# A recurrent mixer's decay factors grown in place by block products, its score grams cut to 32-column groups

## The reference

```python
b = jnp.cumsum(lc, axis=2)                       # lc: log forget
diff = b[:, :, :, None, :] - b[:, :, None, :, :]
decay = jnp.where(tri, jnp.exp(jnp.where(tri, diff, 0.0)), 0.0)
A = jnp.einsum('bhtd,bhsd,bhtsd->bhts', qc, kc, decay)
o = (jnp.einsum('bhts,bhsv->bhtv', A, vc)
     + jnp.einsum('bhtd,bhdv->bhtv', qc * jnp.exp(b), S))
S = (jnp.exp(b_last[:, :, 0, :])[..., None] * S
     + jnp.einsum('bhsd,bhsv->bhdv', kc * jnp.exp(b_last - b), vc))
```

## Time and profile before

| | |
|---|---|
| median of 3 runs | 1780.14 us |
| the profiled execution: its time, its span | 1781.3 us, 1779.7 us |
| PE, DVE, ACT, POOL busy | 1709.6, 940.2, 658.2, 307.3 us |
| mean granted PE clock | 0.989 |

### The profile page before, as it was taken

One profiled execution on the slowest core, in us unless ns is written; L12 is line 12 of the kernel. 1 busy time (PEld: TensorE's weight loads), 2 busy tenths in 40 slices (PEclk: granted clock), 3 DMA queues, 4 the chain that ended last, 5 costly groups with the idle time before them and its releaser, 6 DMA issues.

```text
span 1779.7 us, 33926 instructions
## 1 busy us (share of the span) xinstructions
PE 1709.6 (96%) x12754; PEld 1619.7 (91%) x12754; DVE 940.2 (53%) x1593; ACT 658.2 (37%) x1057; POOL 307.3 (17%) x362
## 2 busy tenths in 40 slices
PE   5999999989999999999999998888899999999997
PEld 5999999969999999999999997555589999999997
DVE  5788888875455555332443434444455555554221
ACT  4544444533433333222333444333333333333111
POOL 3222222212222222000000001111012222221000
PEclk8999999989999999999999999999999999999999
DMA  4222222212222222222233352555613222222331
GB/s 173 62 81 76 72 72 74 70 51 84 87 83 82 82 82 80 82 87 86 91 116 119 97 174 73 184 186 190 197 48 87 84 82 82 82 82 82 106 92 39
DMA packets 79236, 171.76 MB, mean 97 GB/s; under 512 B 6738, under 2 KB 40802, under 8 KB 79170
## 3 DMA queue, kind: packets, MB, share of 16 engines
q1 hardware_dynamic: 73218, 149.84, 27.4%
q0 software_dynamic: 5952, 21.02, 3.4%
HBM read 158.56 MB, written 12.27 MB: 96 GB/s over the span
## 4 chain that ended last, share of the span: by engine, by line
PE 89%; DMA 3%; DVE 2%; issue 2%; ACT 1%; SPq 1%; POOL 0%; DVEq 0%; ACTq 0%; POOLq 0%
PE acc L1353 75%; PE aux L1380 3%; DMA dec_Kd<-cache_k_in 3%; PE acc L1565 2%; PE acc L1583 1%; PE aux L1597 1%; SPq L351 1%; PE aux L1513 1%; PE aux L1441 1%; PE aux L1434 1%; PE aux L1388 1%; DVE xl L713 1%; PE acc L1573 1%; PE aux L1393 1%; PE aux L1419 0%
## 5 line engine op out<-in xcount | busy, mean ns | idle before, releaser
L1353 PE MATMUL acc<-xl,w_hi 128*128 128x288 f32 x2192 | 488.0, 304 | 21.6 <-DVE w_lo L707 16.6
L1353 PE MATMUL acc<-xh,w_hi 128*128 128x288 f32 x2192 | 472.0, 297 | 0.0
L1353 PE MATMUL acc<-xh,w_lo 128*128 128x288 f32 x2192 | 471.6, 297 | 0.0
L707 DVE TENSOR_TENSOR w_lo<-w_raw,w_hi 128x1024 fp32r<-128x1024 f32 (+1 forms) x217 | 283.6, 1307 | 337.6 <-ACT w_hi L382 334.2
L1353 PEld LDWEIGHTS acc<-xl,w_hi 128*128 128x128 f32 x2192 | 355.2, 190 | 35.1 <-DVE w_lo L707 17.3
L1353 PEld LDWEIGHTS acc<-xh,w_lo 128*128 128x128 f32 x2192 | 355.8, 190 | 0.0
L1353 PEld LDWEIGHTS acc<-xh,w_hi 128*128 128x128 f32 x2192 | 355.7, 190 | 0.0
L382 ACT ACTIVATE w_hi<-w_raw 128x1024 fp32r<-128x1024 f32 (+1 forms) x217 | 224.2, 1033 | 240.3 <-PE acc L1353 206.0
L1353 PE MATMUL acc<-ffn_glo,w_hi 128*128 128x288 f32 x704 | 151.0, 295 | 0.0
L1353 PE MATMUL acc<-ffn_gh,w_lo 128*128 128x288 f32 x704 | 149.8, 293 | 0.0
L1353 PE MATMUL acc<-ffn_gh,w_hi 128*128 128x288 f32 x704 | 148.9, 293 | 0.0
(11 more groups left out here) (250 smaller groups left out, 2449.6 us busy)
## 6 DMA issues: line engine op xcount, KB each, us to landing
w_raw<-w_fi_in SPq DMA_DIRECT2D x88, 512.0 KB, 3.6
w_raw<-w_mix_in SPq DMA_DIRECT2D x32, 512.0 KB, 3.6
w_raw<-w_fo_in SPq DMA_DIRECT2D x32, 512.0 KB, 3.5
dec_Kd<-cache_k_in SPq DMA_DIRECT2D x32, 512.0 KB, 6.9
dec_Vd<-cache_v_in SPq DMA_DIRECT2D x32, 512.0 KB, 5.9
w_raw<-w_kv_in SPq DMA_DIRECT2D x17, 512.0 KB, 3.7
w_raw<-w_o_in SPq DMA_DIRECT2D x16, 512.0 KB, 3.6
w_raw<-w_qg_in SPq DMA_DIRECT2D x16, 512.0 KB, 3.6
```

What stands on the lines that cost most here:

```text
L707: nc.vector.tensor_tensor(w_lo[:, pos.slot % SPL, 0:width], w_raw[:, pos.slot, 0:width], w_hi[:, pos.slot % SPL, 0:width].bitcast(F32), AL ...
L1353: mm = nc.tensor.matmul(acc[:, tp, hf, 0:HALF], W[:, sp_, 128 * j:128 * j + 128], X[:, kt, HALF * hf:HALF * hf + HALF], start=(first and j ...
```

## The change

The cumulated logs, their scan, differences and exponentials go. ACT makes f = exp(log f) once a head (`forget`, tile fd). On DVE the factors grow from level to level: `grow` multiplies, in place, k of each left block by the whole decay of the right block and qd (q times f at first) of each right block by the whole decay of the left one, and a third product makes the decays of blocks twice as long (tile dk). After seven levels qd is q exp(b) and k is k exp(b_last - b), so eb and kd go too. The levels now come in the order 1, 2, 4, ... 64, and gram g is k with qd as they stand after g-1 growths. Since a level below 32 has its pairs inside 32 tokens, grams 0 to 5 compute only the diagonal 32x32 blocks, each of the four in its own group of 32 columns of PE, into a narrow tile Ad (`take`, 160 or 128 columns); `diagonal_blocks` moves Ad into A later; grams 6 and 7 compute just the blocks beside it, which are copied without a mask. The samples ride along in grams 0 to 3. All grams and their evaluation use one PSUM bank. `grow` overwrites what gram g reads, so it stands behind `take` g, and gram g+1 waits for it (z_ok). The places in `quarters`, the state products and `new_state` move, and the state products now wait for og.

```diff
 
+        DK_AT = {1: 0, 2: 0, 4: 288, 8: 432, 16: 504, 32: 536, 64: 552, 128: 560}
+
+        def decay(par, m):
+            n = (T if m <= 8 else SEQ) // m
+            return fd[:, par, :] if m == 1 else dk[:, DK_AT[m]:DK_AT[m] + n]
...
+            def forget(t, par):
+
+                act.wait_ge(lf_ok, t + 1)
+                wait(act, z_ok, 8 * (t - 1))
+                nc.scalar.activation(fd[:, par, :], fl[:], ACT.Exp).then_inc(fd_ok, 1)
+                act.wait_ge(kd0_ok, t + 1)
+                wait(act, kT_ps, t - 1)
+                nc.scalar.activation(k_[:, par, :], kd0[:], ACT.Exp).then_inc(k_ok, 1)
...
-            def diff(hd, rp, j):
...
-            def zed(hd, rp, j):
...
+            def grow(hd, rp, j):
+
+                m = 1 << j
+                kv, qv = level(k_[:, rp], m), level(qd[:, rp], m)
+                n = kv.shape[1]
+                dm_ = decay(rp, m)[:, 0:2 * n].rearrange("p (n two) -> p n two", two=2)
+                dve.wait_ge(z_ok, 8 * hd + j + 1)
+                wait(dve, dk_ok, 7 * hd + j)
+                if j == 0:
+                    dve.wait_ge(fd_ok, hd + 1)
+                nc.vector.tensor_tensor(kv[:, :, 0, :], kv[:, :, 0, :], dm_[:, :, 1:2].to_broadcast([P, n, m]), ALU.mult)
+                nc.vector.tensor_tensor(qv[:, :, 1, :], qv[:, :, 1, :], dm_[:, :, 0:1].to_broadcast([P, n, m]), ALU.mult)\
+                    .then_inc(z_ok, 1)
+                if m == 4:
+                    wait(dve, s0_mul, hd)
+                if m == 64:
+                    wait(dve, s_step, 4 * hd)
+                nc.vector.tensor_tensor(decay(rp, 2 * m).rearrange("p (n one) -> p n one", one=1)[:, 0:n],
+                                        dm_[:, :, 0:1], dm_[:, :, 1:2], ALU.mult).then_inc(dk_ok, 1)
 
             def take(hd, g):
 
                 wait(dve, gram_used, 8 * hd + g)
-                dve.wait_ge(gram_ps, 8 * hd + g + 1)
+                dve.wait_ge(gram_ps, 8 * hd + max(g + 1, 2))
                 nc.vector.sem_inc(taking, 1)
-                mk = masks[:, g:g + 1, :]
-                if g in SAMPLE_GRAM:
-                    nc.vector.copy_predicated(As[:], masks[0:NS, SAMPLE_GRAM[g], 0:NS], aux[0:NS, 2, P - NS:P])
-                nc.vector.copy_predicated(A[:], mk.to_broadcast([P, NCH, P]),
-                                          aux[:, g % 2, :].rearrange("p (c s) -> p c s", c=NCH)).then_inc(gram_used, 1)
+                if g < 6:
+                    n = NCH + (g < 4)
+                    at = 160 if g == 1 else 0
+                    nc.vector.copy_predicated(Ad[:, 0:n, :], masks[:, g:g + 1, :].to_broadcast([P, n, 32]),
+                                              aux[:, 1, at:at + 32 * n].rearrange("p (c s) -> p c s", c=n)).then_inc(gram_used, 1)
+                elif g == 6:
+                    for x in (0, 2):
+                        r = slice(32 * x, 32 * x + 32)
+                        tc = nc.vector.tensor_copy(A[r, :, 32 * x + 32:32 * x + 64],
+                                                   aux[r, 1, 0:P].rearrange("p (c s) -> p c s", c=NCH))
+                    tc.then_inc(gram_used, 1)
+                else:
+                    nc.vector.tensor_copy(A[0:64, :, 64:128], aux[0:64, 1, 0:256].rearrange("p (c s) -> p c s", c=NCH))\
+                        .then_inc(gram_used, 1)
+
+            def diagonal_blocks(hd):
+
+                dve.wait_ge(gram_used, 8 * hd + 6)
+                wait(dve, o_ps, hd)
+                for x in range(4):
+                    r = slice(32 * x, 32 * x + 32)
+                    nc.vector.tensor_copy(A[r, :, r], Ad[r, 0:NCH, :])
+                for x in range(2):
+                    r = slice(32 * x, 32 * x + 32)
+                    tc = nc.vector.tensor_copy(As[r, r], Ad[r, NCH, :])
+                tc.then_inc(a_ok, 1)
 
...
-                    new_state(1)
                     dve.wait_ge(oh_ok, td + 1)
                     nc.vector.tensor_tensor(tile_of(ol, td), og[:], tile_of(oh, td).bitcast(F32), ALU.subtract)\
                         .then_inc(ol_ok, 1)
                 if rec:
-                    take(hd, 0)
+                    take(hd, 3)
+                    grow(hd, rp, 2)
+                if tail:
+                    new_state(0)
                 if front:
+                    wait(dve, fd_ok, t)
                     logsig(fr, fl, f_t, lf_ok, t)
-                    dve.wait_ge(lf_ok, t + 1)
-
-                    nc.vector.tensor_tensor_scan(b_[:, par, :], keep[:], fl[:], 0.0, ALU.mult, ALU.add).then_inc(b_ok, 1)
                 if rec:
-                    take(hd, 1)
-                    zed(hd, rp, 2)
-                    diff(hd, rp, 3)
+                    take(hd, 4)
+                    grow(hd, rp, 3)
                 if front:
                     wait(dve, q_ok, t)
                     scaled(qr[:], b0 + 1, 1, qr_ok)
                     dve.wait_ge(qr_ok, t + 1)
                     nc.vector.sem_inc(evac, 1)
+                if tail:
+                    new_state(1)
                 if rec:
-                    take(hd, 2)
+                    take(hd, 5)
+                    grow(hd, rp, 4)
+                    diagonal_blocks(hd)
                 if front:
                     lo(Pos(3, t, 4))
-                if rec:
-                    zed(hd, rp, 3)
-                    diff(hd, rp, 4)
-                    take(hd, 3)
-                if front:
                     logsig(qr, ql, q_t, ql_ok, t)
                 if rec:
-                    zed(hd, rp, 4)
-                    diff(hd, rp, 5)
+                    take(hd, 6)
+                    grow(hd, rp, 5)
+                    take(hd, 7)
+                    grow(hd, rp, 6)
                 if front:
                     wait(dve, vT_ps, t)
                     scaled(vT[:], b0 + 2, 0, vT_ok)
                     dve.wait_ge(vT_ok, t + 1)
                     nc.vector.sem_inc(evac, 1)
-                if rec:
-                    take(hd, 4)
-                    zed(hd, rp, 5)
-                    diff(hd, rp, 6)
...
             def gram(hd, rp, g):
 
+                pe.wait_ge(z_ok, 8 * hd + max(g, 1))
                 if g == 0:
                     pe.wait_ge(k_ok, hd + 1)
                     pe.wait_ge(q_ok, hd + 1)
...
+                wait(pe, gram_used, 8 * hd + (0 if g == 1 else g))
+                lhs, rhs = k_[:, rp], q_[:, rp] if g == 0 else qd[:, rp]
+                if g < 6:
+                    at = 160 if g == 1 else 0
+                    for c in range(NCH + (g < 4)):
+                        for x in range(4):
+                            r, s = slice(32 * x, 32 * x + 32), CH * c + 32 * (x if c < NCH else x % 2)
+                            mm = nc.tensor.matmul(aux[r, 1, at + 32 * c:at + 32 * c + 32], lhs[:, s:s + 32], rhs[:, s:s + 32],
+                                                  start=True, stop=True, tile_position=(0, 32 * x))
                 else:
...
+                    m = 32 * (g - 5)
+                    for c in range(NCH):
+                        for x in ((0, 2) if g == 6 else (0, 1)):
+                            r, s = slice(32 * x, 32 * x + 32), CH * c + 32 * x
+                            q = CH * c + (s % CH // m) * m + m
+                            mm = nc.tensor.matmul(aux[r, 1, m * c:m * c + m], lhs[:, s:s + 32], rhs[:, q:q + m],
+                                                  start=True, stop=True, tile_position=(0, 32 * x))
                 mm.then_inc(gram_ps, 1)
...
                 def state(c):
                     pe.wait_ge(vb_ok, td + 1)
+                    pe.wait_ge(og_ok, 2 * td + 2)
                     wait(pe, s1_ok, 2 * td + c) if c else None
...
                 quarters = (
-                    {1: [(tail, outs), (tail, lambda: state(0))], 5: [(tail, onorm)]},
-                    {0: [(tail, lambda: state(1))], 3: [(rec, gram_0)], 6: [(rec, lambda: gram(hd, rp, 1))]},
-                    {0: [(rec, turn_v)], 2: [(rec, lambda: gram(hd, rp, 2))], 5: [(rec, turn_k)],
-                     7: [(rec, lambda: gram(hd, rp, 3))]},
-                    {1: [(rec, lambda: gram(hd, rp, 4))], 3: [(rec, ds)], 4: [(rec, lambda: gram(hd, rp, 5))],
-                     6: [(rec, lambda: gram(hd, rp, 6))]})
+                    {1: [(tail, outs)], 3: [(rec, grams_01)], 5: [(tail, onorm)], 7: [(rec, lambda: gram(hd, rp, 2))]},
+                    {1: [(tail, lambda: state(0))], 2: [(rec, lambda: gram(hd, rp, 3))], 5: [(rec, lambda: gram(hd, rp, 4))],
+                     6: [(tail, lambda: state(1))]},
+                    {0: [(rec, lambda: gram(hd, rp, 5))], 2: [(rec, turn_v)], 3: [(rec, lambda: gram(hd, rp, 6))],
+                     6: [(rec, lambda: gram(hd, rp, 7))]},
```

More of the change, by code:

```diff
@@ L44 @@
 EPS = 1e-6
-LEVELS = [64, 32, 16, 8, 4, 2, 1]
-SAMPLE_GRAM = {3: 0, 5: 5, 6: 6, 7: 7}
+LEVELS = [1, 2, 4, 8, 16]
 RAW = 4
@@ L1468, in mixer @@
                             run(steps)
-                if rec:
-                    gram(hd, rp, 7)
```

156 lines of the change are left out of this document (46 added, 110 removed).

## The result

The changed kernel takes 1803.7 us (1800.9 to 1808.5, 4 runs) against 1780.9 of the kernel before (1779.1 to 1783.3, 4 runs): the ratio is 1.013 (1.011 to 1.015), slower by 23 us where no change had been forecast, and outside the range of 1768 to 1795. The profiled execution has a span of 1802.5 us, 22.8 more than that of before.

What follows compares the result with a forecast made beforehand. TensorE (PE) bounds the mixer loop; behind it PE and DVE alternate. -0.55 us a head gives -4 in the loop, +2.7 behind it: -1.3 in all, 1779 us on the median, no measurable change; range 1768 to 1795.

Steps and rivals of the forecast that it cites:

- What PE is relieved of: Mixer loop: grams lose 9.4 us a head, small-product bursts cost 4.55, so PE is relieved of 4.85 us a head.
- The -0.4 beside it in the sum: Mixer loop: queue entry of two bursts, 0.2 us each, hidden in the waits, so 0.4 us less a head.
- The rival of records that start one after another: Mixer bursts: small products do not start side by side, a record every 27 ns or more, about 1803 us; chance 0.08.
- The wait at gram 4: Mixer loop: PE waits for grow 2, DVE's way being 11.1 us against PE's 9.5; 1.6 us a head.
- At gram 7: Mixer loop: PE waits for grow 5, behind lo, logsig of q and GpSimd's product S1; 2.7 us a head.
- 0.4 for instructions that wait on DVE's own counters: Mixer loop: 0.1 us for each of the four takes and grows on the two ways, 0.4 us more a head.
- the clock only behind the loop (+2): After the loop: where PE idles longer, more runs at the lower clock; 2 us more.
- Call 8: Head 7's recurrence after the loop: the ring takes 28 to 29 us instead of 33.1, so 4.5 us less.
- The last call: Last mixer call: state products stand behind the norm and og, the second behind ol, delaying the gemm; 5.2 us more.
- a head above 44 us: Sign of being wrong: a mixer-loop head above 44 us, where 42.4 to 43.3 would show the prediction right.
- the first gemm over ol: Sign of being right: it starts 42.2 us after the last projection block, against 39.5 before.
- DVE's ring is longer: Mixer loop: short DVE instructions and waits cost 0.1 us more each, or GpSimd stops one grow a head; 1787 us; chance 0.25.

Runs made afterwards that it cites:

- run 5: Changed kernel with gram 6, take 6 and grow 5 early, diagonal-block moves late, and take 3 and grow 2 ahead of ol: 1767.3 us, ratio 0.993.
- run 1: Changed kernel with only logsig of q moved behind take 6 and grow 5 in DVE's order: 1783.9 us, ratio 1.002.
- run 2: Changed kernel with gram 6, take 6 and grow 5 early and the moves of the diagonal blocks late: 1777.3 us, ratio 0.998.
- run 3: Changed kernel with take 3 and grow 2 ahead of ol instead of behind it: 1803.8 us.
- run 7: Kernel before, with PE made to wait once a head behind gram 3 for one added SyncE transfer: 1798.3 us, ratio 1.009.
- run 8: Kernel before, with PE made to wait once a head behind gram 3 for two added transfers, one behind the other: 1821.0 us, ratio 1.022.
- run 6: The kernel of run 5 with PE's mixer loop written out: 1764.7 us, ratio 0.991.
- run 9: The kernel of run 6 with the second half of the samples' products in outs and the one over As a gemm step later: 1762.9 us.
- run 10: The kernel of run 6; last call's state products around the norm, new_state ahead of og and ol; GpSimd's Vb after grow 6 in call 8: 1755.3 us, 0.985.
- run 11: The changes of run 9 and run 10 together on the kernel of run 6: 1754.2 us, ratio 0.985.
- run 4: Changed kernel with only PE's mixer loop written out: 1797.9 us, ratio 1.010.
- run 12: Kernel before with only PE's mixer loop written out: 1780.3 us, ratio 0.999.

## Why the prediction was wrong

**Up to the end of the last projection block** the forecast was -4 us; it is +11.6 (349.65 to 361.28). By its steps:
- *What PE is relieved of*, 4.85 a head: 4.33 (43.34 less the 39.01 of run 5, where no wait and no low clock is left). The bursts with their surroundings cost 5.0 instead of 4.55: the term mis-sized is the round of 32 columns, 42 ns instead of 28 (from 8 rounds in 0.385 to 20 in 0.89). The -0.4 beside it in the sum (0.2 of entry to each burst, hidden in the waits), for which the text gave no row, did not come: the head from 157.81 to 202.66 us, 44.85 less its waits of 2.95 and 1.11 and 1.5 of back edge, leaves 39.3, not less than 39.01. Seven heads: -30.3 instead of some -37. The rival of records that start one after another, by a rule of at least 25 ns between starts, did not come true: 40 records in 0.50 us are 12.5 ns each. That its number, about 1803, is the one measured is chance; it had bursts of 9.2 us a head.
- *The wait at gram 4*, 1.6 (PE's own terms add to 9.6 and not 9.5, so 1.5): 1.2. *At gram 7*, 2.7: 3.0. Together 27 us in seven heads, for the 30 of the text. Cause and place were right, shown by runs 1 to 3, which moved each away; GpSimd's part was in the walk and is there.
- *0.4 for instructions that wait on DVE's own counters*: not to be seen; 2.8 too much.
- *The step that failed* is the one that is missing. The text priced each wait at its length and charged the clock only behind the loop (+2). In the loop the waits cost the clock too: a mean of 0.96 and about 8 us (a head of run 2, 40.27, and the 3.0 of the wait at gram 7 make 43.3; the heads lie above that, less their back edges, by 1.2, 0, 1.5, 1.6 and 1.2, and the first, which has two stretches, by 2.8). For the stretches behind the wait at gram 7 the cause is shown from both sides: with the wait shorter or gone they go (runs 1, 2), with idle time put into the kernel before such stretches come (runs 7, 8). They are three of the six. For the three behind outs it is open: they too are absent from the traces of runs 1 and 2, but came back in runs 5, 6, 9, 10 and 11, where PE never waits in a head. So 4 to 5 of the 8 us are the price of the waits, and the rest is low clock whose cause is not shown.
- *Back edges*: +3.4 (1.77 and 2.13 us from one pair's start to the next, where 0.265 is usual). The text counted 256 records for 72 as time on PE, not as code. Runs 4 and 6, without the jump, have no such gap, and the shorter body of before has none with it (run 12 gains nothing): it is the jump in the long body.
- Sum: -30.3 + 27 + 1.7 for three short waits in the first head + 8 + 3.4 = +10; 1.6 us stay open.

**Behind it** the forecast was +2.7; it is +8.5. Call 8 gained 2.6 us instead of 4.5 (33.2 to 30.7), as grow 6 ran into GpSimd's Vb: the walk had GpSimd only at S1. The last call lost 8.7 (6.4 to 15.05) where 5.2 and a part of the 2 for the clock were meant, and the gemm up to the norm another 2.4 (59.8 us for 57.4), its first nine pairs being 0.48 apart. The queue behind ol was rightly named, and run 10 shows it; its price was low since the rows were read at the full clock: the clock was at 1.2 GHz up to 394.8 us and again from 398.2 to 411.9, and ol was done 13.2 us behind the start of outs, where the text's way has 10.0. The remaining 2.7 us of the two spans lie in the attention: PE's longer wait for the key cache (3.75 us for 1.20; 1.2 us more over the six such waits) and the low clock behind it. The change doesn't touch that stage, and its waits for the cache (7.3 to 12.2 us in all) and stretches of low clock differ from trace to trace, with those of the unchanged mixer too (runs 7, 8 and 12): no effect of the change can be read from it.

Of the signs of being wrong that the text names, a head above 44 us came (44.5 to 46.7), and the first gemm over ol starts 45.7 us behind the last block where it has 42.2. The rival "DVE's ring is longer" had the right sign for another reason: DVE's work was 27.7 us a head, less than the 30 named, and its ring as long as walked.

## What to carry to other kernels

A wait of 2 to 3 us on a TensorE that was always busy can cost more than its length: here a stretch at half clock, 1.3 to 1.6 us, came behind four of six such waits in run 7 and three of seven in the changed kernel. Price it. So a change that trades PE time for waits has to be summed with both, and a ring in which each step waits for the next wants every other engine's work out of it; here the same products in another order, with PE's loop written out, are 27 us faster than before instead of 23 slower. And count what a loop body holds in instructions when you cut matmuls into smaller ones.
